# Levels 1 to 4 of a block inverse as a loop on TensorE, with the keys' projection regrouped

## What is computed

```python
def step(S, inp):
    r_t, w_t, k_t, v_t, kk_t, a_t = inp
    s_kk = jnp.einsum('zbhvk,zbhk->zbhv', S, kk_t)
    S = (S * w_t[..., None, :] - s_kk[..., None] * (kk_t * a_t)[..., None, :]
         + v_t[..., :, None] * k_t[..., None, :])
    return S, jnp.einsum('zbhvk,zbhk->zbhv', S, r_t)
```

## Time and profile before

| | us |
|---|---|
| median of 3 runs | 2413.44 (2410.11 to 2413.53) |
| the profiled execution | 2407.78, its span 2406.0 |
| six inverses, of which five with key chunks | about 44 to 45 each |

### The profile page before, as it was taken

One profiled execution on the slowest core, in us unless ns is written; L12 is line 12 of the kernel. 1 busy time (PEld: TensorE's weight loads), 2 busy tenths in 40 slices (PEclk: granted clock), 3 DMA queues, 4 the chain that ended last, 5 costly groups with the idle time before them and its releaser, 6 DMA issues. The chain is left out here.

```text
span 2406.0 us, 55446 instructions
## 1 busy us (share of the span) xinstructions
PE 2251.7 (94%) x23172; PEld 1272.4 (53%) x23172; DVE 935.2 (39%) x1965; ACT 397.8 (17%) x685; POOL 167.5 (7%) x162
## 2 busy tenths in 40 slices
PE   5998999999899789999999999889998999999997
PEld 2446776777676765544444444545555444444444
DVE  2356666666667621311111111479513111111113
ACT  2022323232323211100000000211312000000001
POOL 1001010100001000000000000000000000000000
PEclk8998999999999999999999999999999999999999
DMA  9971010101010026699999999602036999999995
GB/s 371 388 310 32 3 33 3 33 3 34 4 33 21 4 66 246 241 384 396 396 391 397 393 395 392 212 1 71 1 140 247 396 396 394 393 396 392 392 391 172
DMA packets 181704, 539.12 MB, mean 224 GB/s; under 512 B 12545, under 2 KB 54145, under 8 KB 181410
## 3 DMA queue, kind: packets, MB, share of 16 engines
q1 hardware_dynamic: 175202, 515.16, 55.6%
q0 software_dynamic: 6336, 21.63, 3.8%
HBM read 510.81 MB, written 25.95 MB: 223 GB/s over the span
## 5 line engine op out<-in xcount | busy, mean ns | idle before, releaser
L2053 PE MATMUL ps<-raw,xs 128*64 128x512 f32 x3072 | 670.9, 594 | 4.5 <-PEq L2047 4.5
L2053 PEld LDWEIGHTS ps<-raw,xs 128*64 128x64 f32 x3072 | 217.1, 137 | 429.1 <-issue 427.7
L2065 PE MATMUL ps<-raw,xs 128*32 128x256 f32 x6144 | 342.5, 380 | 2.2 <-PEq L2047 2.2
L2065 PEld LDWEIGHTS ps<-raw,xs 128*32 128x32 f32 x6144 | 195.2, 110 | 133.1 <-issue 9.8
L2244 DVE SCALAR_TENSOR_TENSOR h<-h,ps 128x768 f32<-128x768 f32 x32 | 30.6, 955 | 461.1 <-DVEq L2243 461.1
L898 PE MATMUL ps<-h,wk 128*128 128x512 f32 (+1 forms) x576 | 175.3, 444 | 1.5 <-PEq L1165 1.3
L1590 DVE COPY_PREDICATED wk<-m,ps 128x128 f32<-128x128 uint8 x360 | 102.3, 352 | 127.5 <-DVEq L1586 126.7
L898 PEld LDWEIGHTS ps<-h,wk 128*128 128x128 f32 x576 | 93.3, 190 | 76.5 <-issue 73.9
L2371 PE MATMUL ps<-h,raw 128*128 128x512 f32 (+1 forms) x448 | 124.0, 438 | 7.2 <-PEq L2362 7.2
L2172 ACT ACTIVATE h<-ps 128x768 f32<-128x768 f32 x32 | 26.0, 812 | 591.6 <-ACTq L2171 591.6
L1025 PE MATMUL ps<-wk 64*64 64x64 f32 x2400 | 108.7, 226 | 9.3 <-issue 7.9
(11 more groups left out here) (331 smaller groups left out, 2563.8 us busy)
## 6 DMA issues: line engine op xcount, KB each, us to landing
raw<-in_moe_w_gate SPq DMA_DIRECT2D x64, 2048.0 KB
raw<-in_moe_w_up SPq DMA_DIRECT2D x64, 2048.0 KB
raw<-in_moe_w_down SPq DMA_DIRECT2D x64, 2048.0 KB
wk<-in_mod_w SPq DMA_DIRECT2D x24, 2048.0 KB, 11.1
wk<-in_ev_w_in SPq DMA_DIRECT2D x18, 512.0 KB, 5.4
raw<-in_od_w_in SPq DMA_DIRECT2D x4, 2048.0 KB, 17.7
hrow<-rows SPq DMA_DIRECT2D x10, 512.0 KB, 3.0
ysum<-low SPq DMA_DIRECT2D x10, 512.0 KB
```

What stands on the lines that cost most here:

```text
L2053: last = pe.matmul(ps[to:to + CAPS, bank_of(kind, ee)], XS[ee][:, c, 0:CAPS], raw[:, slot(l, 2 * m + c // 4), c % 4, 8 * to:8 * to + 512], ...
L2065: last = pe.matmul(ps[to:to + 32, bank_of(kind, ee) + 1, 0:256], XS[ee][:, c, CAPS:], raw[:, slot(l, 2 * m + c // 4), c % 4, 8 * to:8 * to ...
```

## The change

TensorE's 30 turns are written as level 0, then a hardware loop of four turns (`pe.Fori(0, LEVELS - 2)`), one turn for each of the levels 1 to 4, then level 5. Since all turns of a loop run the same instructions, the banks can no longer alternate with the step number: they alternate with the group, `zbank(g)` and `mbank(g)`. Groups 4 and 0, which follow each other across a level's end, so share their banks. The waits are rewritten to fit: `correct(0)` takes four counts of `x_new`, so it stands until the copies of groups 3 and 4 of the level before are done, and `middle(0)` takes two counts of `yw_copied`, those of groups 3 and 4. The eight chunks of the keys' projection go out of the levels 1 to 4: chunks 0 to 3 are issued in level 0 and chunks 4 to 7 in level 5. ScalarE copies the projected keys behind step 25, one step later. VectorE's and GpSimd's instructions and their order stay; every matmul of the inverse is still made.

```diff
-            zbank = lambda q: (4, 6)[q % 2]
+            zbank = lambda g: (4, 6)[g % 2]
+            mbank = lambda g: 2 + g % 2
...
-                        for q in range(NZ + 2):
-                            if q < NZ:
-                                correct(q)
-                            if 0 <= q - 2 < NZ - NT:
-                                middle(q - 2)
...
-                            if following and q % 3 == 2 and q < 3 * KC:
-                                project(K, 0, (q // 3,))
+                        first_correct(0)
+                        first_correct(1)
+                        pe.wait_ge(sem("yvar_read"), 1).then_inc(sem("yvar_read"), -1)
+                        take("x_new", 2)
+                        first_correct(2)
+                        middle(0)
...
+                            project(K, 0, (0, 1))
+                        take("x_new", 2)
+                        first_correct(3)
+                        middle(1)
...
+                            project(K, 0, (2,))
+                        take("x_new", 2)
+                        first_correct(4)
+                        take("yw_copied", 1)
+                        middle(2)
...
+                            project(K, 0, (3,))
+                        with pe.Fori(0, LEVELS - 2) as lev:
+                            take("x_new", 4)
+                            correct(0)
+                            take("yw_copied", 1)
+                            middle(3)
+                            correct(1)
+                            take("yw_copied", 1)
+                            middle(4)
+                            take("x_new", 2)
+                            correct(2)
+                            take("yw_copied", 2)
+                            middle(0)
+                            take("x_new", 2)
+                            correct(3)
+                            middle(1)
+                            take("x_new", 2)
+                            correct(4)
+                            take("yw_copied", 1)
+                            middle(2)
+                        take("x_new", 4)
+                        correct(0, False)
+                        take("yw_copied", 1)
+                        middle(3)
...
+                            project(K, 0, (4,))
+                        correct(1, False)
+                        take("yw_copied", 1)
+                        middle(4)
...
+                            project(K, 0, (5, 6))
+                        take("x_new", 2)
+                        correct(2, False)
+                        take("yw_copied", 2)
+                        corner_middle(0)
...
+                            project(K, 0, (7,))
...
-                            if u == 3 * KC:
+                            if u == NZ - NT:
```

More of the change, by code:

```diff
@@ L1000, in heads, with take @@
                         old_state(0, 1)
[L1002 to L1020, removed]
+                        def take(name, n):
+                            pe.wait_ge(sem(name), n).then_inc(sem(name), -n)
@@ new lines, in diagonal, with first_correct @@
+                        def diagonal(ap, lo, hi):
+                            return ap[lo:hi, :, :, 0, lo:hi].rearrange("p z h n -> p (z h) n")
+                        def first_correct(g):
+                            zb = zbank(g)
+                            for k, (lo, hi) in enumerate(HALF):
+                                to, te = HALF[1 - k]
+                                pe.matmul(ps[to:te, zb, 0:4 * HD].rearrange("p (u n) -> p u n", u=4), eye64[lo:hi], diagonal(mat[:, g], lo, hi), start=True, stop=True)
@@ new lines, in first_correct, with correct @@
+                            last.then_inc(sem("z_ready"), 1)
+                        def correct(g, both=True):
+                            zb = zbank(g)
+                            for z in range(2):
+                                for hh in range(2):
+                                    for lo, hi in HALF:
+                                        pe.matmul(ps[lo:hi, zb, slotT(z, hh):slotT(z, hh) + HD], yw[lo:hi, g, z, hh], invT(g, z, hh, lo, hi), start=True, stop=True)
+                                    for k, (lo, hi) in enumerate(HALF):
+                                        if both or k != z:
+                                            to, te = HALF[1 - k]
+                                            last = pe.matmul(ps[to:te, zb + 1, slotN(z, hh):slotN(z, hh) + HD], invT(g, z, hh, lo, hi), yw[lo:hi, g, z, hh], start=True, stop=True)
@@ L1032, in correct, with middle @@
                             last.then_inc(sem("z_ready"), 1)
[L1034 to L1038, removed]
+                        def middle(g):
                             for z in range(2):
@@ new lines, in heads @@
+                        correct(2, False)
+                        take("yw_copied", 2)
+                        corner_middle(0)
+                        if following:
+                            project(K, 0, (7,))
+                        take("x_new", 2)
+                        correct(3, False)
+                        corner_middle(1)
+                        take("x_new", 2)
+                        correct(4, False)
+                        take("yw_copied", 1)
+                        corner_middle(2)
```

56 lines of the change are left out of this document (26 added, 30 removed).

## The result

The changed kernel takes 2420.06 us (median of 14 runs, 2415.13 to 2425.06) against 2410.47 us for the kernel before (14 runs, 2405.1 to 2417.51): 1.0036 times as long, 95% interval 1.0025 to 1.0047. So it is slower by 0.36%, some 8.7 us by this ratio (the two medians lie 9.6 us apart), where 2425 was forecast. The profiled execution took 2424.84 us, with a span of 2423.0 us and a mean granted clock of 0.978.

A forecast was written before the change was run, and what follows sets the result against it. TensorE, busy 94% of the span, was taken as the bound, with stalls for instruction supply. Five pairs at -3.5 + 7.4 - 0.7 = +3.2 us and the last at -3.8 gave +12.2 on 2413.4: 2425 us, range 2410 to 2437.

The forecast's parts named there:

- The supply of instructions: TensorE's inverse idles for instruction fetch; looping levels 1 to 4 spares 34 of 118 portions, 3.5 us per pair with chunks.
- The rival that these idles are not the supply's: TensorE's "issue" idles in the inverse have another cause and stay: 2450 us, chance 0.09.
- The rival that the body is fetched anew each turn: Loop of levels 1 to 4: every turn fetches its instructions again, some 12 us per pair, 2498 us, chance 0.05.
- No cost for a loop's turn: At the end of each loop turn on TensorE nothing is charged; exposed in all 24 turns it would be 2.6 us.
- The added waits: TensorE's waits from shared banks at the level tops, at `middle(0)` and within levels 1 and 2: together 7.4 us per pair.
- The 0.8 us for the pieces of the steps 5 and 11: Within levels 1 and 2, VectorE's tail pieces make TensorE wait 0.6 and 0.2 us per pair.
- tops of 0.7 or less: Sign against the forecast: TensorE's waits on `x_new` at level tops, expected near 1.9 us at level 2, 1.4 at level 5.
- The value of the loop in a pair: In the first five pairs the loop saves 3.5 us, leaving an inverse of 41.1 us without supply stalls.
- the faster rival: VectorE's tail pieces do not show; only 0.7 us at four tops remains, so 2400 us; chance 0.26.
- The last pair: The last inverse, which carries no chunks, goes to 40.0 us from 43.8: -3.8 us.
- The 1.3 us that I added for the portion behind the loop: Last pair, after the loop: small matmuls use up an instruction portion faster than it comes, 1.3 us.
- The moved chunks and the keys behind them: Chunks in levels 0 and 5 give -0.7 us per pair; later keys cost 0, with about 2 us of slack.

The follow-up runs named there:

- chunks_only: Kernel before with only the eight key chunks moved to levels 0 and 5 and ScalarE's key copy one step later, turns written out: 2440.99 us, ratio 1.0116.
- written_out: Changed kernel with the loop's four turns written out instead of looped, all else the same: 2452.12 us, 1.0158 times the kernel before.
- two_levels: Changed kernel with a loop of two turns of two levels each, banks alternating with the step number again: 2413.24 us, 1.0009 times the kernel before.
- order_turned: pieces_moved with TensorE's order at level ends turned to middle(3), correct(0), middle(4), correct(1): 2396.97 us, 0.9938 times the kernel before.
- pieces_moved: Changed kernel with VectorE's eight tail pieces behind the copies of steps 2, 3, 4, 9, 14, 19 and 24: 2409.37 us, 0.9995 times the kernel before.
- banks_only: Kernel before with only the banks shared by group and the waits this needs, no loop, chunks still spread: 2420.92 us, ratio 1.0036.

## Why the prediction came out as it did

**The supply of instructions: right.** 84 portions and 1.38 MB, as worked out; "issue" idles nearly gone; 125 or 126 matmuls per portion in before, chunks_only and written_out alike. The rival that these idles are not the supply's falls with written_out and chunks_only. The rival that the body is fetched anew each turn falls with the 84 portions, and with the 95 of two_levels, whose body is nearly four portions long. The rule in the Trainium skill, "Runtime: NRT & Kernel Launch", section "Instruction fetch mechanics", read as a window of two pages, does not describe TensorE here.

**No cost for a loop's turn: right for this kernel, not in general.** In the changed kernel a turn's end falls into the wait at the top and can't be told from it. In order_turned that wait is mostly gone. `middle(1)` of two turns of its second inverse:

```profile
354.39 0.46 PE L1043 MATMUL ps<-wk 64*64 64x64 f32 x10
...
359.35 0.46 PE L1043 MATMUL ps<-wk 64*64 64x64 f32 x10
```

The turn takes 4.96 us, five steps at 0.94 take 4.70. The 0.26 are what the loop's turn and the rest of the shared banks cost together. The trace shows how they divide. The loop's branches on TensorE's instruction stream (PEldq), in order_turned:

```profile
L1085 PEldq COMPARE_BRANCH  x24: 76/208/231, 237.2 to 816.8; - x24
```

The 18 branches that are taken last 207 to 231 ns, the six that leave the loop 76, where the prediction cites 108 for each. Between `middle(2)` and `middle(3)`, where the turn ends, the starts of two neighbouring matmuls lie 159 to 212 ns apart in 17 of the 18 turns (109 in one), but at most 71 where the loop is left, with the same two waits ahead. So a turn costs some 0.1 to 0.16 us where no longer wait covers it, about 2 us in all.

**The added waits: right in place, too large in size; this is the mis-sized term.** I charged 7.4 us per pair. The brackets read 1.55, 0.34, 0.68 and 1.03 at the four tops where I had 1.9, 0.7, 1.0 and 1.4, and, in the second pair, three times 0.20 at `middle(0)` where I had four times 0.4. A bracket reads less than a wait costs, though. The profile counts TensorE as busy until the last matmul's end, and one matmul lasts 218 ns while the next starts 20 ns after it (200 in 4.00 us, in the windows of order_turned above). A line of the changed kernel, over all of `middle`:

```profile
L1043 PE MATMUL ps<-wk x2400: 216/218/267, 224.9 to 845.2; 64*64 64x64 f32 x185
```

So a bracket of 0.34 is a gap of some 0.54 in the stream: the matmul at 363.16 starts 0.56 us after the one ahead of it. The turns bear it out: five steps of 0.94, the two brackets of the turn, and 0.20 more for each of them. From 357.43 to 363.16 that is 4.70 + 0.20 + 0.34 + 0.40 = 5.64, and it took 5.73; to 369.16 it is 4.70 + 0.20 + 0.68 + 0.40 = 5.98, and it took 6.00; to 375.50 it is 6.33, and it took 6.34. With that added the tops cost 3.6 + 4 x 0.2 = 4.4 against my 5.0, and `middle(0)` 3 x 0.4 = 1.2 against 1.6. The 0.8 us for the pieces of the steps 5 and 11 are nearly gone: in the second pair no semaphore wait stands there. Sum 5.6 in the second pair, not 7.4. It is 5.6 in the fifth too; the pairs 1, 3 and 4 have a fourth wait at `middle(0)` and one of 0.21 at `correct(3)` in level 1, and come to 6.1 to 6.4. One sign of being wrong, tops of 0.7 or less, came true at the levels 3 and 4 as the profile counts (0.34 and 0.68), not at 2 and 5.

**The value of the loop in a pair: a little too large.** 41.1 + 5.6 - 0.7 is 46.0; it took 46.9. Most of the 0.9 is a stall of the first turn, which still has to be fetched: the 0.60 of "issue" at 353.18, 0.8 with what the pipeline hides, in a stretch to which I gave no cost. So in the second pair two errors of opposite sign, 1.8 and 0.9, leave +2.2 us per pair for the forecast 3.2; that they partly cancel is luck. That the faster rival's threshold of 5.0 us was so near (5.6 measured) is why it had a real chance; pieces_moved shows what it would have taken, since without the pieces at the tops the sign is open again.

**The last pair: right in sign, -5.4 for -3.8.** The 1.3 us that I added for the portion behind the loop did not come: 0.22 us of "issue" at 849.08 is all that stands there. Without it my 38.7 meets 38.4 and 38.1, again in part by luck: the ten waits there come to 5.9 us of brackets, 7.9 with 0.2 more for each, where 6.7 + 2.2 = 8.9 were charged, and the rest of that inverse is longer than reckoned by nearly as much.

**The moved chunks and the keys behind them: right.** The gaps between the inverses are 70.4 to 72.5 us (before 70.5 to 71.2, in its second profile up to 72.3). The fourth gap, 1.2 us longer than in the first profile of before, is over the microsecond that I named as a sign of being wrong; the second profile of before has 72.3 there too, so the change needn't be its cause. GpSimd's last shift and VectorE's use of the shifted keys in the changed kernel's second pair (L1427 and L1478 are the old L1376 and L1427), the answer to the earlier trace rows:

```profile
386.02 0.26 POOL L1427 COPY x<-x 128x2 f32<-128x2 f32 x1
```

```profile
389.08 0.82 DVE L1478 SCALAR_TENSOR_TENSOR x<-x 128x640 f32<-128x640 f32 x1 [0.45 <-DVEq L1477]
```

2.8 us lie between them, where I had about 2, so the cover held.

**Together:** five times 2.2 less 5.4 is +5.6 in the inverses where I had +12.2, and the kernel is 8.7 us slower by the ratio instead of 12. The likeliest case came, nearer to its lower end. The 3 us between 5.6 and 8.7 are not the mechanism's as far as any run shows, so the total meets the forecast better than the mechanism does. Of the 5 us between 2425 and 2420.06 some 3 are the base, 2410.47 in 14 runs for 2413.44 in three.

By the runs of the parts, the change is a trade of three: the banks' waits (+7.8 alone) and the regrouping (+31.2 alone) together cost 45.0 without the loop, and the loop gives 39.6 of that back.

## What to carry to other kernels

Where an engine shows "issue" idles in a long written-out stretch of small instructions, hold its rate against the bytes of its instruction queue: a loop pays where the queue sets the pace, and large instructions spread among small ones do much of the same service without a loop (the five pairs with chunks had 1.4 to 2.8 us of "issue" each, 5.2 to 8.4 with the chunks moved out). A loop takes away what alternated over its turns; count the waits that the shared buffers bring, and look at the order around the loop's end and at the work queued ahead of the releasing copy before judging it, since here those two were worth 23 us of the inverses (272.7 to 249.7) and made a slower kernel a faster one. When a wait is read from a timeline, add what the pipeline hides: here 0.2 us to each.

## What the runs showed that was not expected

A wait of TensorE behind pipelined matmuls costs about 0.2 us more than the profile's bracket (0.34 is 0.54), as the three turns above show. The instruction supply makes up arrears while the engine stands at a semaphore: in banks_only 12.4 us of "issue" vanished behind 20 us of semaphore waits. A loop body of 3.75 portions is still not fetched again in its second turn, but the inverses keep 14.8 of the 46 us of "issue" that they have without a loop, all of them in the first turn, which has to be fetched. And a taken branch of the loop lasts some 0.21 us on TensorE's stream, of which at most some 0.16 cost time where no wait hides it.
